# Fourteen value rows of the small group move from TensorE to VectorE, and its row steps are spread anew

## The reference, cut to what matters

```python
def block(xb):                                   # 128 tokens
    q = (xb @ w_q).reshape(128, 8, 2, 128)
    s1, s2 = einsum(q[:, :, 0], keys1), einsum(q[:, :, 1], keys2)
    v1, i1 = top_k(s1, 16); v2, i2 = top_k(s2, 16)
    sv, si = top_k(all sums v1 + v2, 16)         # per token and head: 16 experts of 16384
    e = i1[si // 16] * 128 + i2[si % 16]
    g = softmax(sv)
    act = gelu(einsum('thkd,td->thk', u_tab[e], xb))
    return einsum('thk,thkd->td', g * act, v_tab[e])
y = rmsnorm(x + block(rmsnorm(x)))
```

## Time and profile before

| | us |
|---|---|
| median of 3 runs | 3907.44 (3903.29 to 3908.87) |
| the profiled execution | 3898.97 |
| its span | 3897.2 |
| PE busy | 2977.0 (76%) |
| DVE busy | 2629.8 (67%) |
| POOL busy | 1433.1 (37%) |
| ACT busy | 560.0 (14%) |
| DMA | 1278 MB, 328 GB/s on a mean |
| L1376, dots of the small group, x160 | 364.4, 2284 ns each |
| L1385, value rows on DVE, x256 | 601.6, 2350 ns each |
| L1788, value rows on PE, x256 matmuls | 181.2 |
| L635, gathers of u_tab, x544, and of v_tab, x288 | 897.7 and 527.4 |

### The profile page before, as it was taken

One profiled execution on the slowest core, in us unless ns is written; L12 is line 12 of the kernel. 1 busy time (PEld: TensorE's weight loads), 2 busy tenths in 40 slices (PEclk: granted clock), 3 DMA queues, 4 the chain that ended last, 5 costly groups with the idle time before them and its releaser, 6 DMA issues.

```text
span 3897.2 us, 32153 instructions
## 1 busy us (share of the span) xinstructions
PE 2977.0 (76%) x10622; PEld 1821.6 (47%) x10622; DVE 2629.8 (67%) x3962; ACT 560.0 (14%) x1106; POOL 1433.1 (37%) x862
## 2 busy tenths in 40 slices
PE   6999988999978999996942222334169899999993
PEld 5989976555544555553521111212143334444441
DVE  3830034899877765465649899899976566665657
ACT  4520011222200000001010001223250000000000
POOL 0000002232344433243336666667522234433334
PEclk9999989999989999997976665666589999999997
DMA  7867757787699989897869999999758999999998
GB/s 197 238 187 240 242 178 272 240 300 267 244 362 383 384 331 383 283 350 290 329 266 392 390 391 385 361 379 366 290 195 354 361 408 420 421 421 421 421 421 353
DMA packets 461518, 1278.18 MB, mean 328 GB/s; under 512 B 24104, under 2 KB 335144, under 8 KB 335912
## 3 DMA queue, kind: packets, MB, share of 16 engines
q0 software_dynamic: 120528, 875.29, 56.0%
q1 hardware_dynamic: 327808, 390.63, 29.6%
q10 hardware_dynamic: 13064, 10.87, 0.8%
HBM read 1265.55 MB, written 12.00 MB: 328 GB/s over the span
## 4 chain that ended last, share of the span: by engine, by line
PE 39%; DMA 32%; DVE 17%; issue 7%; POOL 3%; ACT 1%; ACTq 0%; DVEq 0%; POOLq 0%; SPq 0%
PE ps L1615 25%; DMA region<-in_v_tab_dram,region 19%; PE ps L1599 11%; DVE region L1451 8%; DMA region<-in_u_tab_dram,region 4%; DMA region<-in_w_in_dram 4%; POOL region L635 3%; DVE region L1385 2%; DMA region<-in_w_q_dram 2%; DMA region<-scores_kept 1%; DVE region L1475 1%; DMA region<-in_w_b_dram 1%; PE ps L1810 1%; DVE region L1334 1%; DVE region L1331 1%
## 5 line engine op out<-in xcount | busy, mean ns | idle before, releaser
L635 POOL DMA_INDIRECT region<-in_u_tab_dram,region x544 | 897.7, 1650 | 1778.5 <-DVE region L1376 562.1
L1615 PE MATMUL ps<-region,region 128*128 128x160 f32 (+1 forms) x5120 | 1212.6, 399 | 85.5 <-DMA region<-in_w_in_dram 36.0
L1615 PEld LDWEIGHTS ps<-region,region 128*128 128x128 f32 x5120 | 847.9, 194 | 441.6 <-DMA region<-in_w_in_dram 46.9
L1451 DVE SCALAR_TENSOR_TENSOR region<-region,region 128x2048 f32<-128x2048 f32 x384 | 867.2, 2285 | 93.8 <-DMA region<-in_u_tab_dram,region 56.0
L1385 DVE SCALAR_TENSOR_TENSOR region<-region,region,region 128x2048 f32<-128x2048 f32 x256 | 601.6, 2350 | 480.5 <-DMA region<-in_v_tab_dram,region 474.1
L1840 PE MATMUL ps<-region,region 128*128 128x512 f32 x2048 | 896.7, 600 | 37.4 <-DMA region<-in_v_tab_dram 36.7
L635 POOL DMA_INDIRECT region<-in_v_tab_dram,region x288 | 527.4, 1831 | 666.7 <-DVE region L1385 610.5
L1840 PEld LDWEIGHTS ps<-region,region 128*128 128x128 f32 x2048 | 392.4, 192 | 541.1 <-issue 486.9
L1599 PE MATMUL ps<-region,region 128*128 128x160 f32 (+1 forms) x2048 | 477.5, 395 | 8.3 <-DVE region L1324 4.1
L1788 PE MATMUL ps<-region,region 128*128 128x512 f32 x256 | 181.2, 873 | 327.6 <-DMA region<-in_v_tab_dram,region 323.9
L1599 PEld LDWEIGHTS ps<-region,region 128*128 128x128 f32 x2048 | 336.1, 191 | 146.3 <-issue 8.2
(11 more groups left out here) (217 smaller groups left out, 1403.4 us busy)
## 6 DMA issues: line engine op xcount, KB each, us to landing
region<-in_w_in_dram SPq DMA_DIRECT2D x256, 512.0 KB, 4.7
region<-in_v_tab_dram SPq DMA_DIRECT2D x128, 1024.0 KB, 9.1
region<-in_w_out_dram SPq DMA_DIRECT2D x64, 512.0 KB, 4.6
region<-in_w_q_dram SPq DMA_DIRECT2D x64, 512.0 KB, 6.9
region<-in_w_a_dram SPq DMA_DIRECT2D x32, 512.0 KB, 4.9
region<-in_w_b_dram SPq DMA_DIRECT2D x32, 512.0 KB, 4.8
region<-in_u_tab_dram,region POOLq DMA_INDIRECT x544, 9.7
region<-in_x_prompt_dram SPq DMA_DIRECT2D x7, 1024.0 KB, 9.5
```

The costliest lines, as they stand in the source:

```text
L635: pool.indirect_dma_start(out=slot, out_offset=None, in_=rows_ap, in_offset=bass.IndirectOffsetOnAxis(ap=idx[:, k:k + 1], axis=0)).then_in ...
L1451: stt(out=u_b[s], in0=u_b[s], scalar=1.0, in1=xn_tile(UNITS_A + u), op0=ALU.mult, op1=ALU.mult, accum_out=dots[u % 2][:, k:k + 1]).then_in ...
L1615: last = mm(outs[n][:, 0:WIDTH[g]], wide[s][:, q, n * P:(n + 1) * P], rhs(k), start=(k == 0), stop=(k == n_k - 1))
```

## The change

ROWS_W becomes ROWS_A - V_LAG = 142, so that every step from 18 on has a value row on DVE. Value rows 128 to 141, the first of the sample tokens, are thereby added on DVE, into xf[1] instead of xf[0]. ROWS_P falls from 32 to 18, and ROW_AT puts them at about every twelfth row step of the third stage. STEPS_2 to STEPS_4 are moved: the ranges have 34, 66, 20 steps in loop, gates and output stage, and 26 at norm and queries, where they had 32, 72, 22 and 20. STEPS_1, the slots and POOL's loop stay.

```diff
@@ -62,10 +62,10 @@
 UNITS_A = HEADS + 2
 UNITS_B = 3 * HEADS
 ROWS_A = UNITS_A * TOPK
-ROWS_W = 8 * TOPK
+V_LAG = TOPK + 2
+ROWS_W = ROWS_A - V_LAG
 ROWS_1, ROWS_B = 2 * P, 3 * P
 SLOTS_U, SLOTS_V = 3, 2
-V_LAG = TOPK + 2
 VALUE_AT = {V_LAG + v * (ROWS_A - V_LAG) // ROWS_W: v for v in range(ROWS_W)}
 ROWS_P = ROWS_A - ROWS_W
 ROW_AT = [m * (ROWS_1 - 2 * TOPK) // ROWS_P for m in range(ROWS_P)]
@@ -136,7 +136,7 @@
-STEPS_1, STEPS_2, STEPS_3, STEPS_4 = 14, 46, 118, 140
+STEPS_1, STEPS_2, STEPS_3, STEPS_4 = 14, 48, 114, 134
 STEPS_NORM = (STEPS_4, STEPS_4 + 2)
@@ -1395,7 +1395,7 @@
                     if p in VALUE_AT:
                         v = VALUE_AT[p]
-                        value_row(v, v, v, xf[0])
+                        value_row(v, v, v, xf[v // P])
```

## The result

The changed kernel takes 3932.49 us (median of 5 runs, 3921.49 to 3939.26), the kernel before beside it 3907.44 (5 runs, 3893.06 to 3913.48). The ratio is 1.0064, 95% interval 1.0035 to 1.0093: slower, where 3903 was forecast and 3919 was the end of the range. The profiled execution took 3921.49, its span is 3919.7 (before 3897.2).

The account below looks back on a forecast made before the run. It took DVE to set the loop's end, PE to be busy in gates and queries, and gathers to delay third-stage dots; transfers bound the tail. Second pass +16.7, third stage -21: -4.3 on the 3907.44 median, about 3903 us, range 3884 to 3919.

Parts of the forecast that it names:

- Norm, +13.7: End of the loop: 17 us more DVE work and waits, less 3.3 us of slack, delay the normalisation by 13.7 us.
- Pair 0, -6: First pair of the gates: one dot fewer and a shorter value-row wait before the merge save 6 us.
- Rest of the gates, -3: Gates after the first merge: fewer rows beside the weights shorten the 28.4 us of w_in stalls by 3 us.
- rival 1: Gates bound by transfers: five gathers fewer pay 12.5 us, third stage returns 26; about 3893 us, chance 0.30.
- Output tail, +9: End of the output stage: a route now between add_rows(12) and add_rows(15) lengthens DVE's part to 33 us, costing 9.
- Query, +3: Query stage: DVE's extra rows stay covered, but denser rows compete with w_q loads, costing 3 us.
- Third stage, -21: Third stage: 14 value gathers fewer, each freeing a 2.49 us turn where dots wait, save 21 us.
- Dense tail, 0: Last, transfer-bound stage: same loads in the same order, so no change, 0 us.
- Rival 2: Third stage: u rows alone fill DMA, so only 5 us of waits go; 3919 us, chance 0.17.

Follow-up runs that it names:

- pair0_8: Kernel before with 71 row steps in the gates instead of 72 (8 in pair 0, not 9), one more in the output stage: 3912.33 us, ratio 1.0018.
- steps_alone: Kernel before with only the new row steps (34, 66, 20, 26), still 128 value rows on DVE: 3921.49 us, ratio 1.0062.
- v100_new_steps: Kernel before with 100 value rows in the second pass instead of 128, and the changed kernel's row steps: 3902.45 us, ratio 0.9993.
- values_alone: Changed kernel with the old row steps, so 142 value rows in the second pass: 3913.73 us, ratio 1.0033.
- drop14: Kernel before with 14 of PE's 32 value rows never fetched nor added in the third stage: 3892.1 us, ratio 0.9975.
- after_again: The changed kernel itself, unaltered, timed and profiled once more: 3931.57 us, ratio 1.0079 to the kernel before.
- short_tail: Changed kernel with only the eight gathers of steps 134 to 137 cut to 128 columns: 3926.9 us, ratio 1.0069.
- small_query: Changed kernel with all gathers from step 134 on cut to 128 columns, instructions kept: 3902.67 us, ratio 1.0002.

## Why the prediction was wrong, step by step

The end of the loop, pair 0 and the output tail went as forecast. Three terms failed: the rest of the gates, taken as -3, cost 5 to 14 us in five profiles; the query stage, taken as +3, cost 10.7 to 12.7 in three; and the third stage, taken as -21, returned 7 to 10 in five. In the gates and the queries the step that failed is one and the same: the price of gathers beside weight loads was scaled from PE's visible waits on weights. In the third stage it is the step by which each of the 14 gathers takes its whole turn of 2.49 us off DVE's wait.

**Norm, +13.7:** right, with its mechanism. +14.3, +14.6 and +12.4 in three profiles with the new steps; the slack of 3.3 us was the point from which DVE's work counts.

**Pair 0, -6:** right by itself (-6.9, -9.4, -8.2), but not what it is worth: it brings PE earlier to a stage that is bound by its transfers. pair0_8 bought 8.2 and paid 14.2.

**Rest of the gates, -3:** the first step that failed. The forecast saw PE at 93% and took the 28.4 us on w_in as all that transfers could cost (4.7 more stood on w_a and w_b), scaled by the time in which rows are there. What DMA moves sets the time down to PE's floor of 435: short value gathers take 47.6 us off it, a full gather more or less moves it by 1.7 to 2.8 us. That is rival 1's price of 2.49 for a row, and its argument against itself ("at most 33 us can be had") was wrong too, because PE's busy time contains products slowed by the clock behind late weights. Yet rival 1's time was wrong as well: it counted five gathers fewer as a gain, and the change did move 2.4 MB less, worth 6.8 us at 355 GB/s; the lower rate lost more than that, as 347 GB/s instead of 355 is 11 us on 169.3 MB. No case of the forecast had a lower rate. That steps_alone came out at -3.7 is luck, not support for the -3: its two parts are 25 and 21 us. Why the rate is lower is read from the traces (DVE's waits), not shown.

**Output tail, +9:** right within its bounds (+6.1, +7.0), with its mechanism: 33 us were forecast for DVE's part and 31.0 measured. One reading is off without touching the sum: PE isn't idle for all of the 49 us, it turns blocks at 1746.84 and 1756.75 and makes its first transposes (L1570) at 1790.78.

**Query, +3:** the cover of DVE was judged rightly (12.1 us are left), the price of the transfers wasn't. +10.7 and +12.7; with short gathers -6.4 against before. The waits on w_q rose by only 5.4 us; PE's busy time rose by 5.3 (182.4 against 177.1) at a granted clock of 0.97 in place of 1.00. The forecast took the three visible stalls as the scale of this cost. How dense rows have to be isn't settled: v100_new_steps has 42 gathers in this stage and pays nothing, values_alone has 37 and takes 186.8.

**Third stage, -21:** the mechanism (POOL's stream of gathers, dots waiting late in a burst) was right, the size wasn't. -10.0 in the change, -8.0 in drop14. The u waits fell by 14.6, one us a row and not 1.5, and 6.2 us came back as waits for kept scores (2.0 in after_again, 3.6 in drop14). That a freed wait is partly taken up by the next is one reading; but steps_alone, which has all of its gathers there, also waits 2.4 us longer for kept scores than the kernel before, so why they come later stays open. Taking rows away returns 0.6 to 0.7 us each, adding them costs 1.45, so neither measures the other.

**Dense tail, 0:** right.

Rival 2, the slower one, gave 3919 with +16.7 in the second pass and -5 in the third stage. The profile has +34 (with the first pass's 3.7) and -10: its sign was right by another route. Of the 26.8 us between forecast and profile the third stage has 11.0, the gates 8.1 and the query stage 7.7.

## What to carry to other kernels

Ask of a stage how many bytes it moves and how long that takes at the rate it has in its best slices, before reading its engines: an engine at 93% that waits for operands can be held up by transfers, and its visible waits are less than what they cost. Work that fills an idle engine isn't free when it brings a transfer of its own into such a stage. And cut a stage's total into its parts before a short test is taken as proof: the right part can be offset by another.

## What the runs showed of the hardware

- Waits of 4.47 and 3.37 us on a weight were followed by stretches at a granted clock of 0.61 and 0.69. Over the gates PE's busy time for the same products was 435.0, 440.9, 445.6 and 449.6 us with 0, 10.1, 20.2 and 33.0 us of waits for weights, at mean clocks of 1.00, 0.99, 0.98 and 0.97; but 447.3 at 0.98 with 40.2 (after), so it isn't the sum of the waits alone.
- In the gates, beside weight loads, an indirect gather of 1 MB (128 rows of 8 KB) more or less moved the stage by 2.2 us (62 value gathers and 56), 2.8 (56 and 50) and 2.6 (56 and 44). With six more gathers of only 128 columns the gates took 485.8 us, against 482.8 and 478.4 without them, which the spread of the profiles doesn't tell from nothing.
- Three stores of 1 MB from ACT's queue held it for 16.7 us (after) to 18.3 (before) beside full gathers, for 6.8 (short_tail) and 7.4 (small_query) beside short ones, and ACT's next copy began when the last had been issued.
